# Projection chunks and one scaled copy are moved ahead of waits in three mixers

## The chip, the core and the metric

The kernel runs on one core of one Trainium2 chip. The metric is the device time in microseconds (us) of one execution. The engines go by the names of the profile: PE is the matrix engine (PEld its weight loads), DVE the vector engine, ACT the scalar engine, POOL GpSimd, SP the engine that issues most of the DMAs.

## The reference, cut to what matters

Two small transformer stacks run one after the other on one sequence of 256 tokens of width 1024. Each has two layers, and each layer is a feed-forward block, a mixer and another feed-forward block.

```python
def first_block(x, ...):
    for l in range(DEPTH):
        x = x + 0.5 * m[:, 0, 2] * swiglu(adaln_in(x, ...), w1, w3, w2)
        h = adaln_in(x, norm_g[l, 1], m, 1) @ w_in[l]
        mix = mixer_ab(h, ...) if l % 2 == 0 else mixer_cd(h, ...)
        x = x + m[:, 1, 2] * (mix @ w_out[l])
        x = x + 0.5 * m[:, 2, 2] * swiglu(adaln_in(x, ...), w1, w3, w2)

def mixer_cd(h, ...):
    q, k, v = split_qkv(h, qk_g)
    att = blocked_dense_attention(axial_rope(q), axial_rope(k), v)
    x0, x1, vh = jnp.split(short_conv(h[..., QKV_COLS:], conv_w, conv_b), 3, axis=-1)
    z = x1 * vh
    return jnp.concatenate([att, x0 * (fft_long_conv(z, kfull) + skip * z)], axis=-1)

def hybrid_ab_mixer(u, ...):          # the mixer called hy
    qa, ka, va, cq, kb, vb, k_idx, w_idx = jnp.split(u @ w_in, ...)
    o_a = dilated_mixture(qa, ka, va, table)
    cq = rmsnorm_2(cq, cq_g)
    o_b = dsa_attention(cq @ wq_b, kb, vb, cq @ wq_idx, k_idx, w_idx, table, topk)
    return concat(o_a, o_b) @ w_out

def swa_sink_mixer(u, ...):           # the mixer called sw
    q, k, v = jnp.split(u @ w_in, ...)
    o, lse = banded_attention(q, k, v, bias, C_WINDOW - 1)
    return (o * sigmoid(lse - sinks)) @ w_out
```

In `dsa_attention` a small indexer scores all keys, the best 64 keys of every query are kept, and attention runs over these alone.

## The kernel before

The program is a list of twelve stages: eight feed-forward stages and the mixers ab, cd, hy and sw. Nothing is reordered by a scheduler: each engine has one function per stage, and the order of the calls in it is the order of its instructions. Engines meet only at semaphores.

**Weights.** All weights stream from memory in blocks of 128 x 1024 floats, three to a triple. ACT rounds a block to bf16 (`own_high`, line 1278, `ring_hi`), DVE subtracts to get the rest (`own_low`, line 1756, `ring_lo`). A product is three bf16 matmuls (`product`, lines 518 to 520). An input projection of 128 columns is one *chunk*: eight products into one of the banks pw0 and pw1 (24 matmuls of 256 columns, or 48 of 128 columns for the chunks with values). A chunk of number 6 and up waits until the chunk that used its bank two before it has been copied out.

**Attention.** Heads go in pairs. Numbers of pairs here are those of their mixer, from 0. Pair p runs through the engines like this:

- PE: `pair_scores(p)` (line 761) writes the scores to pw2 and pssq. It waits until DVE has read the scores of the pair before.
- DVE: `pair_bias(p)` adds the bias and takes the row bound (line 1885; in cd it only takes the maximum, lines 1876 and 1878).
- ACT: `pair_exp(p)` (line 1322, in cd 1315; in sw also `es`, line 1325).
- DVE: `pair_normal(p)` makes a diagonal matrix of the reciprocal sums (lines 1898 and 1904, buffer `gu`). It comes ahead of `pair_bias(p + 1)` in DVE's order.
- PE: `pair_turn(p)` (line 781) transposes and scales. ACT copies the result (`pair_copy`, line 1335), PE multiplies with the values (`pair_values`, line 800), and ACT and DVE split the output (`pair_out`, lines 1343 and 1912).

**cd.** Chunks 6 to 17 feed a short convolution: ACT starts it with a scaled copy (`base(n)`, line 1420, buffer `ucv`, which lies in `biasT`), DVE adds the two outer taps (`taps(n)`, lines 1966 and 1967). After chunk 17 PE runs `z_spectrum(0)` (line 951), whose wait is for the taps of chunk 17, then the values and the turn of later pairs, `z_spectrum(1)`, and the inverse transform.

**hy.** PE runs nine chunks, the indexer's queries (`indexer`), the queries of the second half (`queries_b`, which DVE copies to `qb` at line 2129), then four rounds of `index_scores(r)` (line 1081) each followed by one chunk (9 to 12). ACT applies the relu (line 1493), DVE gathers into `msk` (line 2087) and then takes out the best 64 keys, eight at a time (`take_eight`, lines 2097 and 2101), between its other work; the mask is ready with line 2170 (`mskb`). Pairs 0 to 3 need no mask; each is followed by two chunks (13 to 20). Pair 4 is the first that waits for the mask; chunk 21 stands ahead of its scores and chunk 22 behind them.

**sw.** Six chunks go into six banks. `turn_root` (line 581) brings the norm's root into token order, DVE copies it out as `rsT` (line 1940). PE waits for that, and then runs for p = 0 to 3 one chunk (6 + p), the scores of pair p, the values of pair p - 2 and the turn of pair p - 1.

Of the kernel before, what the change touches and what calls it, by code (L numbers as in the profile page):

```python
# [190 lines left out]
def build(nc, stream, wmod, par, cst, cst0, xT, crow, out):  # L191
    scratch = nc.dram_tensor("bias_rows", (4, 16, 512), F32)
    with ExitStack() as ctx:
# [3 lines left out]
        def sem(name):  # L197
            return ctx.enter_context(nc.semaphore(name))
# [139 lines left out]
        rows_ready, rows_saved, bias_in = sem("rows_ready"), sem("rows_saved"), sem("bias_in")  # L338
        scaled, sum_ready, rsT_mm, rsT_ready = sem("scaled"), sem("sum_ready"), sem("rsT_mm"), sem("rsT_ready")
# [168 lines left out]
        def _(pe):  # L508
# [200 lines left out]
            def chunk(i, kind, n):  # L709

                t, b = FIRST[i] + n // 3, n % 3
                bank = bank_of(kind, n)
                await_triple(t, b + 1)
                if kind == "ab" and n >= 2:
                    pe.wait_ge(proj_evac, evac_no[i] + n - 1)
                if kind == "cd" and 2 <= n < CD_PLAIN + 2:
                    pe.wait_ge(proj_evac, evac_no[i] + n - 1)
                if kind == "cd" and n >= CD_PLAIN + 2:
                    pe.wait_ge(conv_evac, n - CD_PLAIN - 1)
                if kind == "hy" and n >= 6:  # L720
                    m = HY_BANKED.index(n)
                    await_evac(HY_BANKED[m - 2] if m >= 2 else m)
                if kind == "sw" and n >= 6:
                    pe.wait_ge(proj_evac, evac_no[i] + (1, 6, 7, 8)[n - 6])
                if CHUNKS[kind][n] in MIXERS[kind]["values"]:
                    for tt in range(TT):
                        for k in range(KD):
                            m = product(bank[:, tt * P:(tt + 1) * P], hidden(k, slice(tt * P, (tt + 1) * P)),
                                        weights(t, b, k, slice(0, P)), start=(tt == 0 and k == 0), stop=(k == KD - 1))
                            if n and b == tt == k == 0:  # L730
                                m.then_inc(triple_used, 1)
                else:
                    for k in range(KD):
                        if n == 0:
                            pe.wait_ge(h_ready, KD * i + k + 1)
                        m = product(bank[:, 0:S], weights(t, b, k, slice(0, P)), hidden(k),
                                    start=(k == 0), stop=(k == KD - 1))
                        if n and b == k == 0:
                            m.then_inc(triple_used, 1)
                m.then_inc(proj_mm, 1)  # L740
# [124 lines left out]
            def mixer_sw(i):  # L865

                for n in range(6):
                    if n == 3:
                        sumsq_of_sum(i)
                    chunk(i, "sw", n)  # L870
                turn_root(i)
                pe.wait_ge(rsT_ready, 2)
                pe.wait_ge(bias_in, 64)
                for p in range(10):
                    if p < 4:
                        chunk(i, "sw", 6 + p)
                    if p < 8:
                        pe.wait_ge(proj_evac, evac_no[i] + (2, 3, 4, 5, 7, 8, 9, 10)[p])
                        pair_scores(i, "sw", p)
                    if p == 4:  # L880
                        pe.wait_ge(proj_evac, evac_no[i] + 10)
                    out_part(i, "sw", p)
                    if p >= 2:
                        pair_values(i, "sw", p - 2)
                    if 1 <= p <= 8:
                        pair_turn(i, "sw", p - 1)
                merge_rest(i, "sw")
# [197 lines left out]
            def mixer_hy(i):  # L1085

                for n in range(3):
                    chunk(i, "hy", n)
                sumsq_of_sum(i)
                chunk(i, "hy", 3)  # L1090
                chunk(i, "hy", 4)
                cq_sums(i)
                turn_root(i)
                chunk(i, "hy", 5)
                chunk(i, "hy", 6)
                indexer(i)
                queries_b(i)
                for r in range(4):
                    index_scores(r)
                    chunk(i, "hy", 9 + r)  # L1100
                pe.wait_ge(bias_in, 48)
                pe.wait_ge(relu_done, 4)
                for p in range(4):
                    pair_scores(i, "hy", p)
                    chunk(i, "hy", 13 + 2 * p)
                    chunk(i, "hy", 14 + 2 * p)
                    if p >= 2:
                        pair_values(i, "hy", p - 2)
                    if p:
                        pair_turn(i, "hy", p - 1)  # L1110
                for p in range(4, 10):
                    if p == 4:
                        chunk(i, "hy", 21)
                    if p < 8:
                        pair_scores(i, "hy", p)
                    if p < 7:
                        chunk(i, "hy", 18 + p)
                    if p == 7:
                        await_evac(23)
                        await_evac(24)  # L1120
                    out_part(i, "hy", p)
                    pair_values(i, "hy", p - 2)
                    if p < 9:
                        pair_turn(i, "hy", p - 1)
                merge_rest(i, "hy")
# [25 lines left out]
        def _(act):  # L1151
# [255 lines left out]
            def mixer_cd(i):  # L1407

                t = FIRST[i] + 2

                def evac(n):

                    act.wait_ge(proj_mm, proj_no[i] + n + 1)
                    fn(proj[:, CHUNKS["cd"][n], :], pw[n % 2][:, 0:S], ACT.Copy).then_inc(proj_evac, 1)

                def base(n):

                    c = CHUNKS["cd"][n] - 6
                    act.wait_ge(proj_mm, proj_no[i] + n + 1)
                    fn(ucv[:, c, :], pw[n % 2][:, 0:S], ACT.Identity, scale=pa("dcw", 12 + c), bias=pa("dcb", c)).then_inc(conv_base, 1)  # L1420

                def copy_z(h):

                    act.wait_ge(zt_mm, h + 1)
                    fn(ztok[:, :, h * S:(h + 1) * S], acc[:, 1536:2048].rearrange("p (t c) -> p t c", t=TT), ACT.Copy).then_inc(zt_copied, 1)

                act.wait_ge(filt_mm, 12)
                inverse_root("filter", norm_c, pw[2][:], 1.0)
                own_high(i, t)
                for n in range(3):  # L1430
                    evac(n)
                own_high(i, t + 1)
                for n in range(3, 6):
                    evac(n)
                own_high(i, t + 2)
                act.wait_ge(mix_mm, 2)
                inverse_root("cd", sqh[:, 0:5, :], accv[:, 0:5, :], 1.0 / HD)
                for n in range(6, 11):
                    base(n)
                    if n > 6:  # L1440
                        own_high(i, t + 3 + (n - 7) // 3, blocks=((n - 7) % 3,))
                pair_exp(i, "cd", 0)
                base(11)
                own_high(i, t + 4, blocks=(1,))
                base(12)
                own_high(i, t + 4, blocks=(2,))
                pair_exp(i, "cd", 1)
                base(13)
                own_high(i, t + 5, blocks=(0,))
                copy_z(0)  # L1450
                base(14)
                own_high(i, t + 5, blocks=(1,))
                pair_copy(i, "cd", 0)
                pair_exp(i, "cd", 2)
                base(15)
                own_high(i, t + 5, blocks=(2,))
                copy_z(1)
                base(16)
                pair_out(i, "cd", 0)
                own_high(i, t + 6, blocks=(0,))  # L1460
                pair_copy(i, "cd", 1)
                pair_exp(i, "cd", 3)
                base(17)
                own_high(i, t + 6, blocks=(1,))
                pair_out(i, "cd", 1)
                pair_copy(i, "cd", 2)
                own_high(i, t + 6, blocks=(2,))
                pair_out(i, "cd", 2)
                split_high(LEAVE[i][0:1])
                pair_copy(i, "cd", 3)  # L1470
                split_high(LEAVE[i][1:2])
                pair_out(i, "cd", 3)
                split_high(LEAVE[i][2:])
# [985 lines left out]
```

## Time and profile before

| what | value |
| --- | --- |
| median of 3 runs | 1882.22 us (1881.88 to 1882.58) |
| profiled execution | 1879.81 us, of which the profile's span is 1878.0 us |
| PE busy | 1814.9 us, 97% of the span |
| DVE busy | 1396.5 us, 74% |
| ACT busy | 978.6 us, 52% |
| mean granted clock of PE | 0.99 |
| chain of work that ended last | 71% PE, 7% DVE, 2% ACT, 1% issue |
| PE in cd | about 676 to 790 us of the span |
| PE in hy | about 1143 to 1267 us |
| PE in sw | about 1614 to 1694 us |

A row of the timeline gives the start, the duration, the engine, the line, the output and the inputs, the shapes, how many instructions were merged, and in brackets the idle time just before it with what ended it. Matmuls overlap: a bf16 matmul of 256 columns is shown as 0.27 us long, and the next one starts 0.11 us after it. An fp32 matmul shows as two records.

### The profile page before, as it was taken

What the parts mean: (1) busy time and instruction counts of PE and PEld (TensorE: products, weight loads), DVE (VectorE), ACT (ScalarE), POOL (GpSimd) and SP (SyncE); (2) the same over time, 40 slices, a digit from 0 to 9 for tenths busy, and PEclk for the clock granted to TensorE, in tenths of its full rate; (3) what the DMA queues carried; (4) which work ended last, traced back from release to release, by engine and by line L of the source; (5) the groups of instructions that cost most, each with busy time, mean ns of one, the idle gap of its engine ahead of it and who ended that gap; (6) DMA issues with size and microseconds to landing.
All of it is one profiled execution on the core that took longest, in us unless ns stands there. A gap on an engine that the chain in (4) does not pass through costs nothing.

```text
span 1878.0 us, 39173 instructions
## 1 busy us (share of the span) xinstructions
PE 1814.9 (97%) x16608; PEld 1585.3 (84%) x16608; DVE 1396.5 (74%) x2243; ACT 978.6 (52%) x1629; POOL 6.6 (0%) x15
## 2 busy tenths in 40 slices
PE   3999999999999999999999999999999999999998
PEld 2788788888888887788888888888888888878887
DVE  6799867898889977686577667867667766758664
ACT  3444556544654465364465446566446544566443
POOL 0000000000000000000000000000000000000000
PEclk7999999999999999999999999999999999999999
DMA  8999644898599943367756665366665666526661
GB/s 325 365 377 382 228 169 152 310 326 303 181 353 376 349 157 135 137 212 245 239 190 214 203 202 180 102 219 209 202 202 181 218 200 202 171 75 209 216 201 49
DMA packets 84810, 420.91 MB, mean 224 GB/s; under 512 B 9347, under 2 KB 9523, under 8 KB 57851
## 3 DMA queue, kind: packets, MB, share of 16 engines
q1 hardware_dynamic: 82700, 410.46, 62.1%
q0 software_dynamic: 1936, 7.95, 1.2%
q8 instruction: 132, 2.16, 0.5%
q14 instruction: 42, 0.34, 0.0%
HBM read 417.24 MB, written 1.13 MB: 223 GB/s over the span
## 4 chain that ended last, share of the span: by engine, by line
PE 71%; DVE 7%; ACT 2%; issue 1%; DVEq 0%; ACTq 0%
PE pw L518 15%; PE pw L519 15%; PE pw L520 15%; PE acc L518 8%; PE acc L519 8%; PE acc L520 8%; DVE ring_lo L1756 2%; PE acc L781 1%; DVE modw L1645 1%; PE acc L800 1%; PE pw L761 0%; DVE gu L1904 0%; PE pw L951 0%; PE pssq L589 0%; PE acc L566 0%
## 5 line engine op out<-in xcount | busy, mean ns | idle before, releaser
L518 PE MATMUL pw<-h_hi,ring_hi 128*128 128x256 bf16 x3096 | 847.2, 274 | 28.1 <-DVE h_lo L1740 18.7
L519 PE MATMUL pw<-h_lo,ring_hi 128*128 128x256 bf16 x3096 | 846.8, 273 | 0.0
L520 PE MATMUL pw<-h_hi,ring_lo 128*128 128x256 bf16 x3096 | 846.7, 273 | 0.0
L1756 DVE TENSOR_TENSOR ring_lo<-land,ring_hi 128x1024 bf16<-128x1024 f32 x418 | 493.3, 1217 | 37.3 <-ACT ring_hi L1278 37.0
L1278 ACT ACTIVATE ring_hi<-land 128x1024 bf16<-128x1024 f32 x418 | 417.8, 1043 | 47.3 <-PE pw L520 18.0
L518 PE MATMUL acc<-a_hi,ring_hi 128*128 128x256 bf16 (+1 forms) x1408 | 383.7, 273 | 1.1 <-DVE a_lo L1838 1.1
L520 PE MATMUL acc<-a_hi,ring_lo 128*128 128x256 bf16 (+1 forms) x1408 | 383.7, 273 | 0.0
L519 PE MATMUL acc<-a_lo,ring_hi 128*128 128x256 bf16 (+1 forms) x1408 | 383.7, 273 | 0.0
L518 PEld LDWEIGHTS pw<-h_hi,ring_hi 128*128 128x128 bf16 x3096 | 303.7, 98 | 79.5 <-DVE h_lo L1740 20.2
L519 PEld LDWEIGHTS pw<-h_lo,ring_hi 128*128 128x128 bf16 x3096 | 303.9, 98 | 36.3 <-issue 0.3
L520 PEld LDWEIGHTS pw<-h_hi,ring_lo 128*128 128x128 bf16 x3096 | 304.0, 98 | 36.0
L1756 DVE TENSOR_TENSOR ring_lo<-land_d,ring_hi 128x1024 bf16<-128x1024 f32 x209 | 255.4, 1222 | 62.3 <-ACT ring_hi L1278 62.2
L1278 ACT ACTIVATE ring_hi<-land_d 128x1024 bf16<-128x1024 f32 x209 | 217.8, 1042 | 0.2 <-DMA land_d<-stream 0.2
L1298 ACT ACTIVATE a_hi<-gu 128x256 bf16<-128x256 f32 (+1 forms) x176 | 73.3, 416 | 231.3 <-DVE gu L1836 227.5
L1645 DVE SCALAR_TENSOR_TENSOR modw<-modw,condb 128x1024 f32<-128x1024 f32 x144 | 171.1, 1219 | 23.5 <-DMA modw<-wmod 22.8
L1293 ACT ACTIVATE gu<-gu 128x256 f32<-128x256 f32 x88 | 36.7, 417 | 286.7 <-DVE gu L1828 286.7
L518 PEld LDWEIGHTS acc<-a_hi,ring_hi 128*128 128x128 bf16 (+1 forms) x1408 | 137.6, 98 | 18.3 <-DVE a_lo L1838 1.6
L519 PEld LDWEIGHTS acc<-a_lo,ring_hi 128*128 128x128 bf16 (+1 forms) x1408 | 137.6, 98 | 16.0
L520 PEld LDWEIGHTS acc<-a_hi,ring_lo 128*128 128x128 bf16 (+1 forms) x1408 | 137.6, 98 | 16.0
L1838 DVE TENSOR_TENSOR a_lo<-gu,a_hi 128x256 bf16<-128x256 f32 (+1 forms) x170 | 72.3, 425 | 82.0 <-ACT a_hi L1298 82.0
L1828 DVE TENSOR_TENSOR gu<-pw,rs 128x512 f32<-128x512 f32 x88 | 60.6, 689 | 91.1 <-PE pw L520 91.1
L1296 ACT ACTIVATE gu<-pw 128x256 f32<-128x256 f32 x82 | 30.6, 374 | 124.9 <-PE pw L520 124.8
(296 smaller groups left out, 1670.4 us busy)
## 6 DMA issues: line engine op xcount, KB each, us to landing
land<-stream SPq DMA_DIRECT2D x207, 1024.0 KB, 5.7
land_d<-stream SPq DMA_DIRECT2D x209, 512.0 KB, 3.7
modw<-wmod SPq DMA_DIRECT2D x144, 512.0 KB, 6.4
biasT<-bias_rows POOLq DMA_DIRECT2D x3, 1536.0 KB, 10.0
biasT<-bias_rows POOLq DMA_DIRECT2D x1, 3072.0 KB, 17.0
land<-stream SPq DMA_DIRECT2D x4, 512.0 KB, 4.9
cst_s<-cst SPq DMA_DIRECT2D x1, 1792.0 KB, 9.5
x<-xT SPq DMA_DIRECT2D x1, 1024.0 KB, 9.6
```

What stands on the lines that cost most here:

```text
L518: mm(o, lhs[0], rhs[0], start=start, stop=False, skip_group_check=True)
L519: mm(o, lhs[0], rhs[1], start=False, stop=False, skip_group_check=True)
L520: return mm(o, lhs[1], rhs[0], start=False, stop=stop, skip_group_check=True)
L781: m = mm(acc[:, o:o + P], (pb_cd if kind == "cd" else pb)[g % 2][:, a, tt, kt * P:(kt + 1) * P], turner[:, a, tt, :], start=(kt == tt == 0 ...
L1278: fn(ring_hi[:, t % RING, b, :], land[:, t % LAND, b, :] if b < 2 else land_d[:, DOWN_NO[t] % LAND, :], ACT.Copy).then_inc(hi_ready, 1)
L1293: fn(sig[:, j % 2, :], sig[:, j % 2, :], ACT.Silu).then_inc(silu_done, 1)
L1296: fn(sig[0:r, j % 2, :], pw[j % (LAG + 1)][0:r, 0:S], ACT.Silu).then_inc(silu_done, 1)
L1298: fn(a_hi[0:r, j % (LAG + 1), :], act_in[0:r, j % 2, :], ACT.Copy).then_inc(a_hi_ready, 1)
L1645: v.scalar_tensor_tensor(modw[:, k % MODR, :], modw[:, k % MODR, :], 1.0, condb[:], ALU.mult, ALU.mult, accum_out=macc[:, g % 2, k:k + 1]) ...
L1756: v.tensor_tensor(ring_lo[:, t % RING, b, :], land[:, t % LAND, b, :] if b < 2 else land_d[:, DOWN_NO[t] % LAND, :], ring_hi[:, t % RING, ...
L1828: v.tensor_tensor(gu[:, j % 2], pw[j % (LAG + 1)][:].rearrange("p (b s) -> p b s", b=2), rs[:].unsqueeze(1).to_broadcast([P, 2, S]), ALU.m ...
L1838: v.tensor_tensor(a_lo[0:r, j % (LAG + 1), :], act_in[0:r, j % 2, :], a_hi[0:r, j % (LAG + 1), :], ALU.subtract).then_inc(act_ready, 1)
```

## The change

Nothing is added or removed. Five projection chunks, one wait and one copy stand elsewhere in the order of their engine.

```diff
@@ mixer_sw, PE
                 turn_root(i)
-                pe.wait_ge(rsT_ready, 2)
-                pe.wait_ge(bias_in, 64)
                 for p in range(10):
-                    if p < 4:
+                    if p < 4 and p != 2:
                         chunk(i, "sw", 6 + p)
+                    if p == 0:
+                        pe.wait_ge(rsT_ready, 2)
+                        pe.wait_ge(bias_in, 64)
                     if p < 8:
                         pe.wait_ge(proj_evac, evac_no[i] + (2, 3, 4, 5, 7, 8, 9, 10)[p])
                         pair_scores(i, "sw", p)
+                    if p == 1:
+                        chunk(i, "sw", 8)
@@ mixer_hy, PE
                 for r in range(4):
+                    chunk(i, "hy", 9 + r)
                     index_scores(r)
-                    chunk(i, "hy", 9 + r)
                 pe.wait_ge(bias_in, 48)
-                pe.wait_ge(relu_done, 4)
                 for p in range(4):
                     pair_scores(i, "hy", p)
+                    if p == 1:
+                        pe.wait_ge(relu_done, 4)
                     chunk(i, "hy", 13 + 2 * p)
@@
                     if p == 4:
                         chunk(i, "hy", 21)
+                        chunk(i, "hy", 22)
                     if p < 8:
                         pair_scores(i, "hy", p)
-                    if p < 7:
+                    if 4 < p < 7:
                         chunk(i, "hy", 18 + p)
@@ mixer_cd, ACT
                 pair_copy(i, "cd", 1)
+                base(17)
                 pair_exp(i, "cd", 3)
-                base(17)
```

On PE in hy, this is the place behind `queries_b` (the matmuls with `cq_hi`, `cq_lo`); line 1081 of before and 1084 of the changed kernel are `index_scores`, the products into `pw` are chunks. Before:

```order
L519 MATMUL acc<-cq_lo,ring_hi 128x256
L520 MATMUL acc<-cq_hi,ring_lo 128x256
L1081 MATMUL acc<-proj 128x128 x4
L518 MATMUL pw<-h_hi,ring_hi 128x256
L519 MATMUL pw<-h_lo,ring_hi 128x256
```

And now, where all 24 matmuls of chunk 9 come first:

```order
L519 MATMUL acc<-cq_lo,ring_hi 128x256
L520 MATMUL acc<-cq_hi,ring_lo 128x256
L518 MATMUL pw<-h_hi,ring_hi 128x256
...
L520 MATMUL pw<-h_hi,ring_lo 128x256
L1084 MATMUL acc<-proj 128x128 x4
L518 MATMUL pw<-ring_hi,h_hi 128x128
```

Each of chunks 9 to 12 has changed places with the index scores that stood ahead of it.

On PE in hy, at pair 4: lines 761 and 766 are its scores and its mask, the products with `ring_hi` in first place are chunk 22, the others the end of chunk 21. Before:

```order
L519 MATMUL pw<-h_lo,ring_hi 128x256
L520 MATMUL pw<-h_hi,ring_lo 128x256
L761 MATMUL pw<-proj,qb 128x128
L761 MATMUL pssq<-proj,qb 128x128
...
L766 MATMUL pssq<-mskb,anti_b 128x256
L518 MATMUL pw<-ring_hi,h_hi 128x128
```

And now:

```order
L519 MATMUL pw<-h_lo,ring_hi 128x256
L520 MATMUL pw<-h_hi,ring_lo 128x256
L518 MATMUL pw<-ring_hi,h_hi 128x128
...
L520 MATMUL pw<-ring_hi,h_lo 128x128
L761 MATMUL pw<-proj,qb 128x128
```

Chunk 22 has moved ahead of the scores of pair 4.

On ACT in cd, behind the copy of pair 1 (line 1335, now 1340): line 1315 (now 1320) is the exponential of pair 3, line 1420 (now 1425) the scaled copy of chunk 17. Before:

```order
L1278 ACTIVATE ring_hi<-land 128x1024
L1335 ACTIVATE probT<-acc 128x512 x2
L1315 ACTIVATE proj,dn<-pw,nb 128x256 x2
L1315 ACTIVATE proj,dn<-pssq,nb 128x256 x2
L1420 ACTIVATE biasT<-pw,par_s 128x256
L1278 ACTIVATE ring_hi<-land 128x1024
```

And now:

```order
L1283 ACTIVATE ring_hi<-land 128x1024
L1340 ACTIVATE probT<-acc 128x512 x2
L1425 ACTIVATE biasT<-pw,par_s 128x256
L1320 ACTIVATE proj,dn<-pw,nb 128x256 x2
L1320 ACTIVATE proj,dn<-pssq,nb 128x256 x2
L1283 ACTIVATE ring_hi<-land 128x1024
```

The copy has moved ahead of the exponential. The orders of DVE, POOL and SP are what they were.

## Rows read from the trace of the kernel before

**Rows 1.** Waits of PE, whole span: waiter, releaser, total us, times, longest us

```profile
PE pw L951 <- DVE biasT L1967: 2.8, 1, 2.8
PE acc L781 <- DVE gu L1904: 1.6, 1, 1.6
PE acc L800 <- ACT probT L1335: 1.4, 2, 1.2
PE pw L518 <- DVE rsT L1940: 1.2, 1, 1.2
PE pw L518 <- ACT proj L1484: 0.5, 1, 0.5
```

**Rows 2.** Busy time, granted clock (PEclk), DMA by stretch, in cd

```profile
core 0: us, PE busy (x) PEld busy (x) DVE busy (x) ACT busy (x) POOL busy (x), PEclk, DMA share, GB/s
750.00:755.00 5.00, 2.22 (x19) 1.89 (x17) 2.48 (x7) 3.56 (x12) 0.00 (x0) 1.00 0.00 0
757.00:759.00 2.00, 2.00 (x4) 0.88 (x3) 0.35 (x2) 0.00 (x0) 0.00 (x0) 0.50 0.84 266
761.00:770.00 9.00, 9.00 (x46) 5.71 (x43) 7.87 (x14) 3.74 (x6) 0.00 (x0) 1.00 0.01 2
```

**Rows 3.** Timeline of PE in cd, the two spectra and what follows them

```profile
755.00 5.37 PE L951 MATMUL pw<-biasT,cst_s 128*128 128x512 f32 x8 [2.78 <-DVE biasT L1967]
760.30 1.08 PE L800 MATMUL acc<-probT,proj 128*64 128x256 f32 x8
...
763.20 1.88 PE L951 MATMUL pw<-biasT,cst_s 128*128 128x512 f32 x4
...
766.73 1.08 PE L800 MATMUL acc<-probT,proj 128*64 128x256 f32 x8
```

**Rows 4.** Timeline of ACT and DVE in cd, around chunk 17's taps

```profile
747.27 1.12 ACT L1335 ACTIVATE probT<-acc 128x512 f32<-128x512 f32 x2
...
751.23 0.17 DVE L1878 TENSOR_SCALAR nb<-mx 128x4 f32<-128x4 f32 x1
...
753.86 0.48 DVE L1966 SCALAR_TENSOR_TENSOR biasT<-pw,par_s,biasT 128x255 f32<-128x255 f32 x1 [2.45 <-ACT biasT L1420]
754.37 0.48 DVE L1967 SCALAR_TENSOR_TENSOR biasT<-pw,par_s,biasT 128x255 f32<-128x255 f32 x1
```

**Rows 5.** Timeline of PE in hy

```profile
1168.70 0.27 PE L519 MATMUL acc<-cq_lo,ring_hi 128*128 128x256 bf16 x1
1168.81 0.27 PE L520 MATMUL acc<-cq_hi,ring_lo 128*128 128x256 bf16 x1
1170.79 0.45 PE L1081 MATMUL acc<-proj 32*128 32x128 f32 x5 [1.71 <-DVE qb L2129]
...
1220.34 0.34 PE L761 MATMUL pw<-proj,qb 64*128 64x128 f32 x1 [2.05 <-DVE mskb L2170]
...
1239.20 0.37 PE L761 MATMUL pw<-proj,qb 64*128 64x128 f32 x1
```

**Rows 6.** Timeline of DVE and ACT in hy

```profile
1180.65 0.42 DVE L2074 TENSOR_TENSOR proj<-pw,rs 128x256 f32<-128x256 f32 x1 [2.28 <-PE pw L520]
...
1219.77 0.43 DVE L2170 TENSOR_SCALAR mskb<-msk 128x512 bf16<-128x512 f32 x1
...
1222.69 0.48 DVE L1885 CUSTOM_DVE_ANT_0 prob<-pssq,biasT,no_sink 128x256 f32<-128x256 f32 x1
...
1226.76 0.87 ACT L1335 ACTIVATE probT<-acc 128x384 f32<-128x384 f32 x2 [0.91 <-PE acc L781]
...
1238.29 0.48 DVE L1885 CUSTOM_DVE_ANT_0 prob<-pssq,biasT,no_sink 128x256 f32<-128x256 f32 x1
```

**Rows 7.** Timeline of DVE in sw: biases of pairs 3, 4 and 7

```profile
1651.60 0.42 DVE L1930 TENSOR_TENSOR proj<-pw,rs 128x256 f32<-128x256 f32 x1
1652.14 0.35 DVE L1885 CUSTOM_DVE_ANT_0 KR<-pw,biasT,neg_sink 128x128 f32<-128x128 f32 x1
...
1657.08 0.35 DVE L1885 CUSTOM_DVE_ANT_0 prob<-pw,biasT,neg_sink 128x128 f32<-128x128 f32 x1
...
1671.88 0.35 DVE L1885 CUSTOM_DVE_ANT_0 KR<-pw,biasT,neg_sink 128x128 f32<-128x128 f32 x1
```

## The prediction, on record before the run

> **What bounds the kernel now.** PE is busy for 97% of the span and carries 71% of the chain that ended last, so the first view to read is the list of what PE waited for. What the change can touch there is small: the wait of the first spectrum in cd for the taps (2.8 us), one in sw for rsT (1.2) and one for the diagonal matrix gu (1.6) [rows 1], and two in hy, for qb (1.71) and for the mask (2.05) [rows 5]. The second view is the timeline around each of these, on PE and on the engine that ends the wait: it tells whether the waited-for chain itself moves. The third is the table by stretch with PE's granted clock, because one of the pauses is followed by a slow stretch.
>
> A measure for what follows: consecutive bf16 matmuls start 0.11 us apart but are shown 0.27 us long [rows 5], so a pause before one costs PE 0.16 us more than its idle figure. A chunk is 24 such steps, some 2.7 us with the change of bank; the 48 steps at half width of a value chunk come to the same.
>
> **cd: the copy of chunk 17.** Before, ACT finishes the copy of pair 1's turn at about 748.4, waits for the row maximum of pair 3, runs its exponentials and only then the copy of chunk 17, for which DVE has idled 2.45 us. The maximum is there at 751.23 + 0.17 = 751.40 [rows 4]. Moved ahead, the copy fits into ACT's pause between 748.4 and 751.4, and the exponentials start when they did. DVE's order is unchanged, so the taps now follow the maximum at once: they start at 751.43 and not 753.86, which is **2.4 us** earlier, and the spectrum with them (755.00 to about 752.6). Some 0.4 us of the 2.8 us wait is left. What runs behind (values of pair 2, the turn of pair 3) needs ACT's copy of pair 2 and DVE's normal of pair 3; both stand behind the moved copy or the taps and come about 0.45 us earlier, by the length of the copy, which just suffices: I find nothing that is later than PE by more than 0.1 us.
>
> **cd: the clock.** The eight matmuls of the first spectrum take 760.30 - 755.00 = 5.30 us, the eight equal ones of the second 766.73 - 763.20 = 3.53 us [rows 3]. The granted clock says why: it is 1.00 before and after, and 0.50 (1.2 of 2.4 GHz) in 757 to 759 [rows 2]. PE had been idle for 2.78 us. The pauses of 1.71, 2.05 and 1.6 us in the other mixers are not followed by a fall (the mean clock of the whole span is 0.99). With 0.4 us of idleness left I take the fall as gone and count **1.8 us**; its bounds are 0 and 1.8.
>
> **hy: chunks 9 to 12 ahead of the index scores.** PE runs chunk 9 (2.7 us) in the pause for qb, so 1.71 + 0.16 = **1.9 us** of pause go, and the first index scores start 2.7 - 1.9 = 0.8 us later than before. ACT's relu and DVE's gathers start 0.8 us later with them. That costs nothing at the end, because DVE afterwards idled 2.28 us for PE's chunk 11 [rows 6], which now comes earlier: the gathers run through, and the long DVE stretch that ends in the mask starts about 2.2 us earlier. The wait for the four relus, moved behind pair 1's scores, is then some 6 us old. The pause of 0.5 us ahead of chunk 15 (ACT's value copy behind the exponentials of pair 0) [rows 1] shrinks, between 0 and 0.5; I take **0.35**, the difference of 2.2 and 1.9.
>
> **hy: chunk 22 ahead of pair 4.** The mask was ready at 1219.77 + 0.43 = 1220.2; 2.2 us earlier is 1218.0. PE, 2.2 us earlier and with chunk 22 in the pause, comes to the scores at 1220.34 - 1.9 - 0.35 - 2.2 + 2.7 = about 1218.7, later than the mask, so the pause (2.05 + 0.16 = **2.2 us**) goes entirely. But here something else is late next. Before, chunk 22 (2.7 us of PE) stood between the scores of pair 4 and everything that ACT and DVE do for that pair. Now the scores move by only 4.4 - 2.7 = 1.7 us, while PE behind them would be 4.4 us earlier. From the end of pair 4's bias (1222.69 + 0.48) a chain of ACT and DVE runs to pair 6's bias (end 1238.77): exponentials, copy of pair 3, split of a block, bias of pair 5, exponentials, copy, splits, bias of pair 6. It had two slacks: 0.91 us where ACT waited for PE's turn, and 1239.20 - 1238.77 = 0.43 us before pair 7's scores, of which 0.1 is the signal itself [rows 5, 6]. So pair 7's scores can come 1.7 + 0.9 + 0.3 = **2.9 us** earlier, and not 4.4: 1.5 us come back as new waits of PE ahead of pairs 6 and 7. Behind pair 7 I find no second chain that is longer. The term is 2.9 us, with 2.2 (chunk 22 worth nothing) and 4.4 (all pauses filled) as ends.
>
> **sw: chunk 6 ahead of rsT.** It fills the 1.2 us pause whole, since DVE delivers rsT long before the chunk ends. The scores of pair 0 come **1.2 us** earlier and all that hangs on them.
>
> **sw: chunk 8 ahead of the turn of pair 0.** It fills the 1.6 us pause. But sw runs at the pace of another loop: bias of p on DVE, exponentials of p on ACT, normal of p on DVE, bias of p + 1. The bias starts at 1657.08 for pair 4 and 1671.88 for pair 7, 4.93 us apart each time, and 4.94 from pair 3 to 4 [rows 7]; the turns and chunks of PE are not in it. PE waits for it at the end, 1.2 us for ACT's last copies but one [rows 1]. The filled pause therefore comes back as waits for ACT's copies of pairs 0 and later. What is left is that the bias of pair 3 (1652.14, behind a copy begun at 1651.60 and 0.42 long) had waited up to **0.2 us** for PE's scores. Together 1.4 us; ends 1.2 and 1.2 + 1.7 + 0.2 = 3.1.
>
> A page of the Trainium skill (Perfetto Trace Analysis, Optimization Strategy) says to find the gaps between slices of the engine one optimizes for, and to have what they wait on start sooner or finish faster. Taken as it stands it would count every gap, the rival "all filled" below; rows 6 and 7 speak against it.
>
> **Sum.** 2.4 + 1.8 + 2.9 + 1.4 = 8.5 us. The span goes from 1878.0 to 1869.5, the profiled execution from 1879.81 to 1871.3. The median of the runs lies 2.4 us above the profiled execution; with the same distance it goes from 1882.22 to **1873.7 us** (-0.45%). The feed-forward stages between are limited by PE and only start earlier; the splits and their DMAs hang on the same semaphores and move with them.
>
> **Rivals.**
> - *The clock falls all the same*, at the spectrum or at a new short wait. Then 6.7 us, 1875.5 us. For it: the fp32 work of this place is thin, and 0.4 us of waiting is left. Against it: the second spectrum, same work without a pause, runs at 1.00.
> - *All filled.* If the loops behind have more slack than I read, the sum is cd 2.8 + 1.8, hy 4.4, sw 3.1 = 12.1 us, 1870.1 us.
> - *Waits only change places in hy and sw*: hy keeps nothing because the later index scores push the mask, sw keeps its 1.2 us, cd 2.4. Then 3.6 us, 1878.6 us. For it: the relu and gathers do start 0.8 us later. Against it: DVE's 2.28 us pause.
> - *Slower: short waits pull the clock down.* Four short pauses of PE remain or arise in fp32 stretches (cd 0.4, hy two of together 1.5, sw about 1.3). If each brings a fall like the one seen, at 1.8 us each, that is 7.1 us against 6.7 us of gain: 0.4 us slower, 1882.6 us. It decides at whether a pause below 1.7 us is enough; the three present ones say no. The Trainium skill (TensorE: Matmul & The Clock Gate, A second HAM failure mode) tells of a kernel in which frequent small idles between groups of matmuls made the clock swing; no row here shows that.
> - That the change does not do what it says is excluded by the order of instructions shown above.
>
> **Chances.** Forecast (8.5) 0.60; clock falls all the same 0.18; all filled 0.08; waits change places 0.10; slower 0.04. A measurement tells about 0.2% (3.8 us) from no change, so faster means below 1878.5. Faster: the first three and a little of the fourth, 0.88; same 0.10; slower 0.02. The range takes in the first two cases with 1.5 to 2 us of error: 1871.3 to 1877.5.
>
> **What would show it.** cd: taps (lines 1971 and 1972 now) at the end of the maximum without a pause, the first spectrum 3.5 us long, clock 1.00 there. hy: no pause before the index scores and the scores of pair 4, new ones before the scores of pairs 6 and 7, together 1.5 us. sw: no pause at rsT or the turn of pair 0, but one of about 1.3 us for ACT's copy before the values of pair 0, and biases still 4.93 us apart. Wrong would be a bias loop that shortens, a mask later than PE, or a clock of 0.5 in any mixer.

## The result and the profile after

The changed kernel takes 1872.03 us (median of 5 runs, 1871.61 to 1872.78) against 1882.22 us (5 runs, 1880.65 to 1883.69): a ratio of 0.9947, with a 95% interval of 0.9936 to 0.9959. Its profiled execution took 1872.03 us with a span of 1870.2 us. A second measurement on another occasion gave 1872.12 against 1882.20 us, ratio 0.9951 (0.9938 to 0.9965).

The longest waits of PE in hy and then in sw, columns as in [rows 1]:

```profile
PE pw L761 <- DVE nb L1890: 1.2, 1, 1.2
```

```profile
PE acc L800 <- ACT probT L1340: 2.8, 3, 1.3
```

The pauses for qb, the mask, rsT and gu are gone. Two things are new: a pause of PE for a bias (nb) in hy, and more waiting for ACT's copies in sw (three pauses, 2.8 us in all, where [rows 1] has two of 1.4 us in all).

In cd, the timeline of PE at the first spectrum, which answers to [rows 3]:

```profile
753.24 3.67 PE L954 MATMUL pw<-biasT,cst_s 128*128 128x512 f32 x8 [0.23 <-DVE biasT L1972]
756.84 1.08 PE L800 MATMUL acc<-probT,proj 128*64 128x256 f32 x8
```

The pause has shrunk from 2.78 to 0.23 us, and the first spectrum takes 756.84 - 753.24 = 3.60 us instead of 5.30. The stretch that was at a clock of 0.50 in [rows 2] is now at 1.00 (columns as in [rows 2], here and below):

```profile
755.00:760.00 5.00, 5.00 (x30) 3.15 (x29) 4.83 (x11) 2.74 (x7) 0.00 (x0) 1.00 0.50 174
```

The timeline of DVE and ACT at the same place ([rows 4] before):

```profile
752.02 0.17 DVE L1883 TENSOR_SCALAR nb<-mx 128x4 f32<-128x4 f32 x1
752.10 0.48 DVE L1971 SCALAR_TENSOR_TENSOR biasT<-pw,par_s,biasT 128x255 f32<-128x255 f32 x1
752.23 0.48 ACT L1320 ACTIVATE proj<-pw,nb 128x256 f32<-128x256 f32 x1 [2.22 <-DVE nb L1883]
```

The taps follow the maximum without a pause, while ACT still waits for it: the copy of chunk 17 has cost ACT nothing.

**Stage by stage.** PE runs the same matmuls in both kernels, so the start of the same matmul in the two traces, read once in each feed-forward stage, tells what every mixer gave. All kernels of this study are read in this way (us against the first profile of before; minus is earlier; the last column says in which of these three mixers a stretch at a clock of 0.50 lies).

| kernel | up to cd | cd | hy | sw | clock at 0.50 |
| --- | --- | --- | --- | --- | --- |
| changed | +0.8 | -4.2 | -2.9 | -1.5 | none |
| changed_again | +0.4 | -4.2 | -2.9 | -1.5 | none |
| first_of_each | +0.1 | -4.2 | -0.6 | -1.2 | hy |
| second_of_each | +2.0 | 0.0 | -0.8 | -0.2 | cd |
| filled_pause | +1.2 | -1.7 | +1.6 | 0.0 | hy |
| filled_both | +1.5 | -1.7 | 0.0 | +0.1 | none |
| copy_alone | +0.4 | -4.2 | +1.6 | 0.0 | hy |
| late_splits | -0.4 | -4.2 | -4.3 | -1.5 | none |
| half_signal | +1.7 | -4.2 | -2.9 | -4.7 | none |
| half_signal_hy_sw | +2.3 | -4.2 | -4.6 | -4.7 | none |

The column "up to cd" moves by up to 2.7 us between executions of code that is the same up to there; it is not an effect of any edit. A part of it is the clock as well: `second_of_each` and `half_signal_hy_sw` (+2.0 and +2.3) have a stretch at 0.50 at about 216 us that the others do not have, and PE takes 1.7 us longer there up to its next pause (21.8 us for 20.1). The three mixers of the changed kernel together gave 8.6 us.

### The profile page after: what moved, and what is told of

It is laid out like the page before. It is cut to its first block, busy times and chain, and to the rows that moved or that the text cites. A ratio compares the mean times of both kernels' runs of the same rounds, so it can differ in the third digit from the quotient of the medians.

```text
span 1870.2 us, 39173 instructions
## 1 busy us (share of the span) xinstructions
PE 1811.0 (97%) x16608; PEld 1583.5 (85%) x16608; DVE 1396.3 (75%) x2243; ACT 978.0 (52%) x1629; POOL 6.6 (0%) x15
## 4 chain that ended last, share of the span: by engine, by line
PE 70%; DVE 7%; ACT 3%; issue 1%; DVEq 0%; ACTq 0%
PE pw L518 15%; PE pw L519 14%; PE pw L520 14%; PE acc L518 8%; PE acc L519 8%; PE acc L520 8%; DVE ring_lo L1761 3%; DVE modw L1650 1%; PE acc L781 1%; DVE prob L1890 1%; ACT prob L1327 1%; ACT ring_hi L1283 0%; DVE gu L1909 0%; ACT KR L1327 0%; PE pssq L589 0%
```

## The experiments

**One part in each mixer.** The mixers lie hundreds of microseconds apart, so one kernel can test a part of the change in each of them. `first_of_each` takes the copy in cd, chunks 9 to 12 in hy and chunk 6 in sw:

```diff
 # cd, ACT
+                base(17)
                 pair_exp(i, "cd", 3)
-                base(17)
 # hy, PE
+                    chunk(i, "hy", 9 + r)
                     index_scores(r)
-                    chunk(i, "hy", 9 + r)
...
-                pe.wait_ge(relu_done, 4)
                 for p in range(4):
                     pair_scores(i, "hy", p)
+                    if p == 1:
+                        pe.wait_ge(relu_done, 4)
 # sw, PE
-                pe.wait_ge(rsT_ready, 2)
-                pe.wait_ge(bias_in, 64)
                 for p in range(10):
                     if p < 4:
                         chunk(i, "sw", 6 + p)
+                    if p == 0:
+                        pe.wait_ge(rsT_ready, 2)
+                        pe.wait_ge(bias_in, 64)
```

> The kernel before with one part of the change in each mixer: in cd the copy of chunk 17, in hy chunks 9 to 12 ahead of the index scores, in sw chunk 6 ahead of rsT. Chunk 22 (hy) and chunk 8 (sw) stay where they were. Read from the matmuls' starts, stage by stage. My theory (each part is worth its pause as long as no loop of ACT and DVE holds it): cd 4.2 us earlier, hy 2.2, sw 1.2, together 7.6. Rival (waits only change places in hy, the later relus push the mask): hy 0, together 5.4. Rival (hy needs both parts): less than 1.9 in hy.

Measured: one execution of 1873.94 us against 1882.29; cd -4.2, sw -1.2, hy -0.6 and not -2.2. The missing 1.6 us in hy are not the mask coming later. PE's pause for it is as long as it was, but this time the clock falls behind it. A row of the timeline of PE and two of the table by stretch, all of this kernel:

```profile
1214.13 0.55 PE L761 MATMUL pw<-proj,qb 64*128 64x128 f32 x1 [2.05 <-DVE mskb L2172]
```

```profile
1211.50:1214.00 2.50, 0.57 (x6) 0.27 (x3) 2.40 (x11) 0.00 (x0) 0.00 (x0) 1.00 0.00 0
1214.20:1217.40 3.20, 3.20 (x23) 2.42 (x24) 2.08 (x7) 0.00 (x0) 0.00 (x0) 0.50 0.43 92
```

The pause is the 2.05 us of [rows 5], and it ends 1220.34 - 1214.13 = 6.2 us earlier than there, of which 4.1 us come from ahead of hy: the mask itself is some 2.1 us earlier, as forecast. The matmul behind it, 0.34 us long there, takes 0.55 us here. In the profile of before the clock stayed at 1.00 at this place:

```profile
1220.30:1223.50 3.20, 3.16 (x48) 2.83 (x49) 3.12 (x11) 0.29 (x1) 0.00 (x0) 1.00 0.40 79
```

So -2.2 + 1.6 = -0.6. That a fall at this place costs 1.6 us is measured by two kernels below that leave hy as it was (filled_pause and copy_alone, +1.6 each).

`second_of_each` has only the other parts, chunk 22 in hy and chunk 8 in sw:

```diff
 # hy, PE
                         chunk(i, "hy", 21)
+                        chunk(i, "hy", 22)
...
-                    if p < 7:
+                    if 4 < p < 7:
                         chunk(i, "hy", 18 + p)
 # sw, PE
-                    if p < 4:
+                    if p < 4 and p != 2:
                         chunk(i, "sw", 6 + p)
...
                         pair_scores(i, "sw", p)
+                    if p == 1:
+                        chunk(i, "sw", 8)
```

> The kernel before with only chunk 22 ahead of pair 4's scores in hy and chunk 8 ahead of the turn of pair 0 in sw. My theory: in hy PE comes to pair 4's scores 0.5 us later than before, the chain of ACT and DVE to pair 7 has 0.9 + 0.3 us of slack, so 0.7 us earlier remain of the pause of 2.2; in sw the bias loop decides and 0.2 us or less remain of the pause of 1.7; cd unchanged. Together 0.9 us. Rival (all pauses filled): 2.2 + 1.7 = 3.9 us.

Measured: 1880.80 us; hy -0.8, sw -0.2, cd 0.0. The pauses for the mask and for gu are gone from its list of waits (2.05 and 1.56 us of idleness), and two new rows, one in hy and one in sw, show where they went:

```profile
PE pw L761 <- DVE nb L1888: 1.2, 1, 1.2
```

```profile
PE acc L800 <- ACT probT L1338: 2.8, 3, 1.3
```

The two parts of hy are worth 2.2 and 0.8 us alone and 2.9 together. The rival in which every filled pause pays is out: it wanted 2.2 for chunk 22 and 1.7 for chunk 8.

**Is it the pause that makes the clock fall?** `filled_pause` is the kernel before with three additional matmuls in cd whose result nobody reads:

```diff
                 pe.wait_ge(zt_copied, 2)
                 if jt == 0:
+                    for _ in range(3):
+                        mm(acc[:, 1536:2048], cs("C", 0, P), ztok[:, 0, :], start=True, stop=True)
                     pe.wait_ge(conv_evac, 12)
```

> The kernel before, and in cd three additional fp32 matmuls of 512 columns whose result nobody reads, put into PE's pause ahead of the first spectrum (0.86 us each, 2.6 us of the 2.78). The spectrum still starts when the taps are there, at about 755.0. If the pause makes the clock fall, the granted clock stays 1.00 and the eight matmuls of the spectrum take 3.5 us and not 5.3: cd ends 1.8 us earlier although work was added. If the fall belongs to this place or to the fp32 work, the spectrum takes 5.3 us and cd gains nothing.

Measured: 1880.97 us. The timeline of PE, where L947 are the added matmuls:

```profile
753.26 2.74 PE L947 MATMUL acc<-biasT,cst_s 128*128 128x512 f32 x6
756.12 3.70 PE L953 MATMUL pw<-biasT,cst_s 128*128 128x512 f32 x8
```

and its clock there:

```profile
757.00:759.00 2.00, 2.00 (x6) 0.95 (x5) 1.52 (x7) 0.22 (x1) 0.00 (x0) 1.00 0.36 74
```

This stage starts 1.2 us later than in the first profile, so the spectrum starts at the place where it did (755.0 + 1.2 is 756.2), with more work ahead of it, and still cd ends 1.7 us earlier. The pause is the cause of the fall in cd; neither the place nor the fp32 work is. `filled_both` below repeats it. In hy, which is untouched, this execution has the fall (+1.6).

`filled_both` fills the pause for the mask as well, with two such matmuls:

```diff
                         chunk(i, "hy", 21)
+                        await_evac(20)
+                        for _ in range(2):
+                            mm(pw[0][:], cs("C", 0, P), cs("S"), start=True, stop=True)
```

> The kernel before with additional fp32 matmuls whose result nobody reads in two pauses of PE: three ahead of the first spectrum in cd, two (1.7 us) ahead of pair 4's scores in hy. No wait is shortened. If a pause of 2.05 us also lets the clock fall in some executions, though not in the profiled one of before, the falls at both places go: cd 1.8 us earlier in each execution, hy 0 to 1.6 us according to whether the execution of before had a fall there; the median over five rounds is 2.5 to 3.5 us below that of before, and no stretch at 0.50 is in cd or hy. If only the 2.78 us pause counts: 1.8 us. If filling does nothing for the clock in hy: 1.8 us or less.

Measured: 1880.56 us (11 runs, 1878.72 to 1881.44) against 1883.14 us (21 runs, 1878.89 to 1885.35), ratio 0.9988 (0.9979 to 0.9996). The medians are 2.6 us apart, 1.7 of which is the clock in cd. That fits falls in hy that come in part of before's executions, but the interval reaches from 0.8 to 4.0 us and excludes neither of the others. Here the profiles tell more. Of those taken of kernels that still have the 2.05 us pause (before, first_of_each, filled_pause, copy_alone), three of four have the fall behind it. The one profile of `filled_both` has no fall in hy. One of those four lacks it too, so this makes it likely, and does not show as it is shown for cd, that the filling kept the clock up there.

`before_again` was the kernel before itself.

> The kernel before itself, for its spread and a second profile. If falls of the clock come and go with the execution, its times differ by 2 to 3 us among themselves (as 1880.65 to 1883.69 did), and the profile has the fall in cd again and may have one in hy ahead of pair 4. If they belong to the program, the profile has them where the first one has, and hy and sw agree with it within 0.1 us.

Measured: 1883.73 us (11 runs), ratio 1.000 (0.999 to 1.0009); ten of the runs lie between 1879.12 and 1886.05 us. The eleventh, the profiled one, took 3849 us. What stretched it is not known, and its trace holds no change of the clock at all, so it says nothing about the falls. What remains is the spread of the runs, 5 us and more for before and some 2.5 us for the changed kernel, and it goes with the clock. Every run has its mean granted clock on record. Of 47 runs of before, the 20 with a clock of 0.989 or less average 1884.1 us and the 24 with 0.991 or more average 1881.5 us. No run of the changed kernel (ten), of `copy_alone` or of `filled_both` (eleven each) is below 0.990.

**The copy alone, timed.** `copy_alone` is the diff of cd above and nothing else.

> The kernel before with the copy of chunk 17 moved in cd and nothing else. Theory: 2.4 us of the pause and 1.8 us of the clock, 4.2 us in all, ratio 0.9978; the profile shows the first spectrum 3.5 us long and no stretch at 0.50 in cd. If the clock were not part of it, 2.4 us.

Measured: 1877.72 us (11 runs) against 1882.20 us (15 runs), 4.5 us, ratio 0.9975 (0.9966 to 0.9984); cd -4.2 in the profile. That is 2.4 from the wait and 1.8 from the clock, as forecast, and 2.4 alone (0.9987) lies outside the interval. The clock fell in hy:

```profile
1218.00:1221.00 3.00, 3.00 (x31) 3.00 (x30) 2.54 (x9) 1.56 (x7) 0.00 (x0) 0.50 0.82 251
```

**What gives back 1.5 us in hy?** `late_splits` is the changed kernel with two biases moved ahead of block splits on DVE:

```diff
-                own_low(i, t + 9, blocks=(0,))
                 pair_bias(i, "hy", 5)
+                own_low(i, t + 9, blocks=(0,))
...
-                own_low(i, t + 9, blocks=(1, 2))
                 pair_bias(i, "hy", 6)
+                own_low(i, t + 9, blocks=(1, 2))
```

> The changed kernel, and on DVE in hy two biases ahead of block splits: the bias of pair 5 ahead of one split, the bias of pair 6 ahead of two. If the 1.5 us that hy gives back are the chain of ACT and DVE from pair 4 to pair 7, that chain is 1.1 us shorter at pair 6's scores and 2.3 us more at pair 7's, the new waits there go, and hy is 1.5 us earlier than in the changed kernel (4.4 us earlier than before). If another wait stands behind, 0 to 1 us.

Measured: 1869.41 us (one run; the changed kernel 1872.03); hy -4.27 against -2.93, so 1.3 us more. The scores of pair 7 on PE, first in the changed kernel, then in late_splits, where no pause stands ahead of them:

```profile
1232.77 0.37 PE L761 MATMUL pw<-proj,qb 64*128 64x128 f32 x1 [1.23 <-DVE nb L1890]
```

```profile
1230.26 0.37 PE L761 MATMUL pw<-proj,qb 64*128 64x128 f32 x1
```

The scores of pairs 5 and 6 start 6.25 us apart in both kernels, those of pairs 6 and 7 7.60 and 6.31 us. So the chain of ACT and DVE up to pair 7 is what kept 1.3 us of the filled pauses, all of it in this one wait.

**What bounds sw?** `half_signal` is the changed kernel with one more semaphore: DVE signals when the bias of a pair's first head is done, and ACT starts that head's exponentials on it.

```diff
 # ACT, pair_exp
-                act.wait_ge(pair_b, g + 1)
+                halved = kind in ("sw",)
+                if halved:
+                    act.wait_ge(pair_h, g + 1 - pair_no[STAGE_OF[("sw",)[0]]])
+                else:
+                    act.wait_ge(pair_b, g + 1)
...
                 for a in range(2):
+                    if a and halved:
+                        act.wait_ge(pair_b, g + 1)
                     for tt in range(TT):
...
 # DVE, pair_bias, in the loop over a, behind the loop over tt
+                    if a == 0 and kind in ("sw",):
+                        ins.then_inc(pair_h, 1)
                 ins.then_inc(pair_b, 1)
```

> The changed kernel, and in sw DVE signals once more, after the first head of a pair's bias, so that ACT starts its exponentials 0.7 us before the whole bias is done. If sw runs at the pace of the loop bias, exponentials, normal, the distance of the biases goes from 4.93 to about 4.3 us until PE is the slower (4.6 us for a pair), PE's waits for ACT's copies (2.8 us in all) shrink, and sw is 2.0 us earlier than in the changed kernel (1.3 to 2.8). If PE or ACT as such bounds sw, 0 to 0.5 us.

Measured: 1869.79 us; sw -4.7 against -1.5, so 3.2 us more, where I had expected 2.0 and at most 2.8. Starts of the biases of pairs 3, 4 and 7 on DVE, to be read beside [rows 7]:

```profile
1644.33 0.35 DVE L1897 CUSTOM_DVE_ANT_0 KR<-pw,biasT,neg_sink 128x128 f32<-128x128 f32 x1
1648.60 0.35 DVE L1897 CUSTOM_DVE_ANT_0 prob<-pw,biasT,neg_sink 128x128 f32<-128x128 f32 x1
...
1661.39 0.35 DVE L1897 CUSTOM_DVE_ANT_0 KR<-pw,biasT,neg_sink 128x128 f32<-128x128 f32 x1
```

They are 4.27 us apart from pair 3 to 4 and as much on the way to pair 7, not 4.93, and PE waits for ACT's copies only 0.5 us:

```profile
PE acc L801 <- ACT probT L1347: 0.5, 1, 0.5
```

The loop bias, exponentials, normal is the bound of sw in the changed kernel. In `half_signal` PE is the slower, as expected, and at the pace expected: the scores of pairs 6 and 7 start 4.61 us apart, with no wait of PE between them (4.94 us in the changed kernel):

```profile
1655.77 0.37 PE L762 MATMUL pw<-proj 64*128 64x128 f32 x1
...
1660.37 0.37 PE L762 MATMUL pw<-proj 64*128 64x128 f32 x1
```

The 4.6 us for a pair on PE were right. What was too small is the gain, which had been bounded by the waits in the list. From the first scores to the values of pair 0 PE gained 0.8 us, from there to the values of pair 7 2.4 us. The list has only 2.8 - 0.5 = 2.3 us of these 3.2. In the changed kernel the scores of pairs 4 to 7 start 4.72, 4.93 and 4.94 us apart with no wait in the list between them: the loop held PE back there in pauses that are too short for the list.

**Both together.** `half_signal_hy_sw` has the late splits, and the signal in hy as well as in sw.

> The changed kernel with the two biases ahead of the splits in hy and the signal after the first head in hy and sw. Theory: against the changed kernel hy 1.4 us (the splits; the signal finds no PE wait but 0.3 us in hy) and sw 2.0 us earlier, 3.4 together: about 1868.6 us as a median, 0.9928 of before. If the loop is not what bounds sw, 1870.6 us.

Measured: 1867.89 us (5 runs, 1867.42 to 1868.61) against 1883.14 us, ratio 0.9921 (0.9908 to 0.9935). In its profile hy has no wait of PE that the list shows, and sw the 0.5 us above. The 0.7 us beyond the forecast of 1868.6 come from sw, which gave 3.2 us again where 2.0 were forecast. It beats both kernels; its median is 4.1 us below the first one of the changed kernel.

**The changed kernel once more.**

> The changed kernel itself beside before, with more runs of before. The trace's stages give 8.6 us. If the pause of 2.05 us in hy costs the clock in some two thirds of before's executions (two of three profiles), the median is 8.6 + 1.1 = 9.7 us below before, and the times of the changed kernel lie closer together than before's. If the clock in hy plays no part, 8.6 us.

Measured: 1872.12 us (5 runs, 1871.63 to 1874.12) against 1882.20 us (15 runs, 1879.34 to 1884.52), 10.1 us. The mixers gave the same 8.6 us in the profile. The difference of the medians is nearer to 9.7 than to 8.6, but the interval (6.6 to 11.7 us) holds both.

## Why the prediction was right

- **cd, the copy.** Forecast 2.4 us and a rest of 0.4 us; measured 2.5 (755.00 + 0.78 - 753.24, with the 0.78 us by which this execution was late ahead of cd) and a rest of 0.23 us. ACT's pause took the copy in whole, and nothing behind the spectrum was late. Right.
- **cd, the clock.** Forecast 1.8; 5.30 - 3.60 = 1.7 us measured, and `filled_pause` and `filled_both` show that the pause is the cause, since 1.7 us come back when the pause is filled with useless work.
- **hy.** Forecast 2.9 with 1.5 us given back. Measured 2.9, and 2.2 and 0.8 for the two parts alone. I had placed the new waits ahead of pairs 6 and 7; there is one, of 1.23 us, ahead of pair 7, and none ahead of pair 6, whose scores keep their distance. `late_splits` shows that it is this chain: with two biases earlier in it, 1.3 of the 1.5 us come back.
- **sw.** Forecast 1.4, measured 1.5; chunk 8 alone gave 0.2. The biases of pairs 4 to 7 are still 4.93 to 4.94 us apart in the changed kernel. The pause of 1.3 us ahead of the values of pair 0 is where it was put:

```profile
1638.24 0.87 PE L800 MATMUL acc<-probT,proj 128*64 128x256 f32 x8 [1.32 <-ACT probT L1340]
```

- **The sentence that was wrong** is that pauses of 1.71, 2.05 and 1.6 us are not followed by a fall of the clock, and that "the three present ones say no". I had one profile. That same profile also has a stretch at 0.50 from about 226.6 to 230 us, with no pause of PE in the list for the 11 us ahead of it. A fall can thus come without a pause just ahead, a case that the prediction did not weigh. These are PE's small fp32 matmuls ahead of that stretch and the clock across it:

```profile
222.76 3.60 PE L534 MATMUL acc<-biasT,par_s 33*8 33x512 f32 x8
```

```profile
226.00:230.00 4.00, 4.00 (x19) 2.05 (x19) 4.00 (x11) 2.86 (x7) 0.00 (x0) 0.57 0.02 4
```

With the pause of 2.05 us unchanged the fall is there in three of four profiles. The forecast did not suffer: removing this pause also removes a cost of 1.6 us that before's profiled execution happened not to pay. On the average of its executions that is some 1.2 us if three in four hold (an estimate from four profiles).
- **The size.** Forecast 1873.7 us, measured 1872.0. The span went down by 7.8 us (forecast 8.5) because the changed kernel's execution was 0.8 us late ahead of cd. The step that was off is the last one, which carried the 2.4 us between before's profiled execution and its median over to the changed kernel. Its profiled execution is its median. The profiled execution of before was a lucky one; the missing fall in hy explains about half of the 2.4 us, and the part up to cd, which varied by 2.7 us from profile to profile, can hold the rest: by that column before's first profile is the second earliest of eleven, and the changed kernel's is the middle one, 0.8 us later. How the 2.4 us divide was not settled.
- **The rivals.** "The clock falls all the same" did not happen in either profile of the changed kernel. "All filled" is refuted by `second_of_each`, "waits only change places" by `first_of_each` and `second_of_each` for hy (it holds for chunk 8 in sw). Its price of 3.6 us also left out the 1.8 us of the clock in cd without a reason; with them it is 5.4 us. "Slower" had the right mechanism, a fall after a pause below 2.78 us, but the new pauses in hy and sw of 1.2 to 1.3 us showed none in the five profiles that have one or both (changed, changed_again, second_of_each, late_splits, half_signal). So the advice of the Trainium skill that the prediction weighed (Perfetto Trace Analysis, Optimization Strategy), to find the gaps and let their dependencies come sooner, is sound for `late_splits` and `half_signal`, which shorten the loop; filling the gap with other work paid 0.2 of 1.7 us in sw.

## What to carry to other kernels

Moving independent work into a pause of the busiest engine pays only up to the next point at which a loop of the other engines decides; compare the distance of that loop's instructions (here 4.93 us from bias to bias) before and after the pause with what the busy engine needs for one round by itself (here 4.61 us), and if the loop is the longer, shorten the loop instead, by an earlier signal or by moving work that nobody waits for behind what somebody waits for. What the loop holds back can be more than the list of waits shows. A pause of the matrix engine can cost more than its own length, because its clock may be at half rate when it resumes. One profile does not show what such a pause costs on average, so look at several before calling it harmless.

## What the runs showed of the hardware

- The granted clock fell to 0.50 (1.2 GHz) after a pause of 2.78 us in cd in both profiles that have it, and after a pause of 2.05 us in hy in three of four; after those of 1.71 us (for qb), 1.56 us (for gu) and 1.2 to 1.3 us in hy and sw in none. The length of the pause alone does not decide: at about 215 us, ahead of the mixers studied here, PE pauses for a_lo for 2.07 to 2.69 us in seven profiles, and the clock falls behind it in two (2.07 us in `second_of_each`, 2.12 us in `half_signal_hy_sw`) and not in five (2.12 us in the changed kernel, up to 2.69 us in `filled_both`). A fall cost 1.7 to 1.8 us at fp32 matmuls of 512 columns and 1.6 us in hy's mixture.
- The clock also fell with no pause just ahead: in before, `late_splits` and `half_signal` it is at 0.50 for some microseconds from 226 to 228 us on, 12 us after a pause of 1.1 us. There the fall cost nothing: PE's next pause ends 20.1 us behind that one, as in the kernels without it, against 21.8 us in `second_of_each` and `half_signal_hy_sw`.
- Filling the pause in cd with matmuls that nobody reads kept the clock at 1.00 and made the stage 1.7 us shorter, in two profiles of two.
- Without a fall, a mixer repeats to within 0.1 us from execution to execution; what varied is the part ahead of cd, by up to 2.7 us, of which a fall at about 216 us is 1.7 us in two profiles.
